# A hybrid layer with 32 experts: four 2 MB weight chunks asked for in uneven row groups, with later pairs, more halves and expert 2's gather later

## What is computed

```
logits = x @ w_router + b_router            (264 x 32)
gates  = softmax(top 4 of logits)
for each expert e, on the tokens that chose it:
    h   = xb @ w_up[e] + b_up[e]            (1024 -> 2048)
    act = min(h_glu, 7) * sigmoid(1.702 * h_glu) * (clip(h_lin, -7, 7) + 1)
    y   = act @ w_down[e] + b_down[e]       (1024 -> 1024)
out = sum over the 4 experts of gate * y
```

## Time and profile before

| | us |
|---|---|
| median of 3 runs | 1084.72 |
| the profiled execution | 1084.98 |
| its span, first to last instruction | 1083.2 |
| TensorE busy | 1065.1 |
| VectorE busy | 361.6 |
| ScalarE busy | 152.6 |
| granted TensorE clock | 0.998 of full speed |
| data moved | 431.47 MB, mean 398 GB/s |

### The profile page before, as it was taken

The page is one execution under the profiler, slowest core; times in us unless marked ns, Lnnn a source line. Parts: engine busy times, 40 slices in busy tenths (PEclk is TensorE's granted clock), DMA queues, the critical chain, the costliest instruction groups (busy, mean ns, idle before and its releaser), DMA issues.

```text
span 1083.2 us, 13206 instructions
## 1 busy us (share of the span) xinstructions
PE 1065.1 (98%) x5687; PEld 442.8 (41%) x5688; DVE 361.6 (33%) x572; ACT 152.6 (14%) x302; POOL 11.9 (1%) x28
## 2 busy tenths in 40 slices
PE   9999999999999999999999999999999999999997
PEld 7888664333333333333333333333333333333332
DVE  3376444233333222233332222333233232232234
ACT  2121144111111111101111111101111111101113
POOL 1000010000000000000000000000000000000002
PEclk9999999999999999999999999999999999999999
DMA  8875969999999999999999999999999999999994
GB/s 284 310 277 207 404 213 389 400 403 433 427 435 429 429 431 431 430 431 431 428 434 429 425 431 427 431 430 430 430 434 428 428 430 429 425 427 427 428 412 173
DMA packets 44075, 431.47 MB, mean 398 GB/s; under 512 B 4808, under 2 KB 20204, under 8 KB 25712
## 3 DMA queue, kind: packets, MB, share of 16 engines
q1 hardware_dynamic: 43408, 430.41, 95.2%
q10 hardware_dynamic: 608, 0.20, 0.1%
HBM read 427.00 MB, written 3.48 MB: 397 GB/s over the span
## 4 chain that ended last, share of the span: by engine, by line
PE 79%; DMA 20%; issue 0%; ACT 0%; DVE 0%; ACTq 0%; POOLq 0%; DVEq 0%; POOL 0%
PE bank L1027 32%; DMA ring_all<-in_w_down 19%; PE bank L1046 17%; PE bank L708 9%; PE bank L1094 5%; PE bank L1001 4%; PE bank L1038 3%; PE bank L818 2%; PE bank L1009 1%; PE bank L1019 1%; PE bank L1106 1%; PE bank L826 1%; DMA ring_all<-in_w_in 1%; PE bank L1087 1%; PE bank L661 1%; PE bank L1132 1%
## 5 line engine op out<-in xcount | busy, mean ns | idle before, releaser
L1027 PE MATMUL bank<-ring_all,work 128*64 128x512 f32 x2040 | 482.4, 600 | 5.8 <-DMA ring_all<-in_w_up 5.8
L1027 PEld LDWEIGHTS bank<-ring_all,work 128*64 128x64 f32 x2040 | 132.5, 136 | 255.0 <-issue 238.8
L1046 PE MATMUL bank<-ring_all,work 128*64 128x512 f32 x992 | 225.6, 596 | 2.7 <-DMA ring_all<-in_w_down 2.6
L1875 DVE TENSOR_TENSOR h_tok<-h_tok,bank 128x1024 f32<-128x1024 f32 (+1 forms) x67 | 81.7, 1220 | 233.7 <-PE bank L1094 227.9
L1046 PEld LDWEIGHTS bank<-ring_all,work 128*64 128x64 f32 x992 | 68.3, 137 | 133.1 <-issue 132.2
L708 PE MATMUL bank<-work,ring_all 128*128 128x264 f32 x384 | 87.0, 387 | 0.5 <-DMA ring_all<-in_w_in 0.5
L1845 DVE TENSOR_TENSOR work<-bank,bias_up 128x1024 f32<-128x1024 f32 x32 | 39.2, 1224 | 127.6 <-PE bank L1038 127.6
L708 PEld LDWEIGHTS bank<-work,ring_all 128*128 128x128 f32 x384 | 72.4, 190 | 12.9 <-DMA ring_all<-in_w_in 0.9
L1094 PE MATMUL bank<-work 64*128 64x512 f32 (+1 forms) x268 | 75.1, 637 | 0.0
L1862 DVE TENSOR_TENSOR work<-work 128x512 f32<-128x512 f32 x32 | 22.2, 693 | 108.9 <-ACT work L1443 108.8
L1427 ACT ACTIVATE work<-bank 128x264 f32<-128x264 f32 x32 | 12.5, 390 | 322.2 <-PE bank L1019 322.2
(11 more groups left out here) (238 smaller groups left out, 549.5 us busy)
## 6 DMA issues: line engine op xcount, KB each, us to landing
ring_all<-in_w_up SPq DMA_DIRECT2D x36, 4096.0 KB, 28.0
ring_all<-in_w_down SPq DMA_DIRECT2D x24, 4096.0 KB, 33.2
ring_all<-in_w_up SPq DMA_DIRECT2D x47, 2048.0 KB, 38.9
ring_all<-in_w_down SPq DMA_DIRECT2D x11, 2048.0 KB, 41.1
ring_all<-in_w_up SPq DMA_DIRECT2D x17, 1024.0 KB, 8.2
ring_all<-in_w_in SPq DMA_DIRECT2D x13, 1024.0 KB, 5.0
ring_all<-in_w_down SPq DMA_DIRECT2D x10, 1024.0 KB, 7.9
ring_all<-in_w_out SPq DMA_DIRECT2D x4, 1024.0 KB, 11.7
```

What stands on the lines that cost most here:

```text
L1027: mm = pe.matmul(bank[half * CAP:(half + 1) * CAP, up_bank(n) + b, :].rearrange("q (k p) -> q p k", k=KT), x, src[half][:, b * 512:(b + 1) ...
L1046: mm = pe.matmul(bank[half * CAP:(half + 1) * CAP, Y, :], av[:, 2 * i + k, :], src[:, k * D + half * 512:k * D + (half + 1) * 512], start= ...
L1875: tt(rows, rows, bank[0:m, b:b + 2, :], ALU.add).then_inc(comb_added, 1)
```

## The change

- Chunks 10 to 23, instead of 10 to 19, come in halves. The semaphores for first halves are now one per slot, with a count.
- Pairs begin at expert 8 instead of expert 4. Experts 4 to 7 are fetched in singles.
- In experts 8, 14, 20 and 26 (`EVENED`) the second chunk of the up projection is asked for in four transfers: rows 0 to 111; rows 112, 114, ... 126; rows 113, 115, 117; rows 119, 121, ... 127. The first chunk of experts 8 and 14 is for that no longer part of a pair (in 20 and 26 it was single already).
- In expert 1's up projection the gather for expert 2 moves from behind step 1 to behind step 6, the turning of the marks of expert 0 from behind step 5 to behind step 4, and the turning of the gathered rows of expert 2 from behind step 3 into the down projection of expert 0, behind step 1. The transposes of the gates move from up(0) to up(2), behind step 0. ScalarE's list follows.

```diff
-HALVES = 10
-PAIRED = (4, 28)
+HALVES = 14
+PAIRED = (8, 28)
 SPLIT = 16
+EVENED = (8, 14, 20, 26)
+EVEN_ROWS = (slice(0, 112), slice(112, 128, 2), slice(113, 119, 2), slice(119, 128, 2))
...
-                 if s % RING < RING - 1 and not (stream[s][0] == "u" and stream[s][1] >= SPLIT and stream[s][2] == 0)]
+                 if s % RING < RING - 1 and not (stream[s][0] == "u" and stream[s][2] == 0
+                                                 and (stream[s][1] >= SPLIT or stream[s][1] in EVENED))]
+        evened = [place["u", e, 1] for e in EVENED]
...
-            seen[s % RING] += 1
+            seen[s % RING] += len(EVEN_ROWS) if s in evened else 1
             signal.append((s % RING, 16 * seen[s % RING]))
...
-            half_in = [sem(f"half_in{i}") for i in range(HALVES + 1)]
+            half_in = [sem(f"half_in{r}") for r in range(RING)]
...
+            halved = [RING - 1] + [s for s in range(RING, RING + HALVES) if s != RING + STASHED]
+
+            def half_signal(s):
+                return s % RING, 16 * sum(h % RING == s % RING for h in halved if h <= s)
...
-                        fill(s, slice(0, 2 * FF), half_in[s - RING + 1])
+                        fill(s, slice(0, 2 * FF), half_in[s % RING])
...
-                    sp.dma_start(ring(s), chunk_src(stream[s])).then_inc(landed[s % RING], 16)
+                    for part in EVEN_ROWS if s in evened else (slice(0, P),):
+                        sp.dma_start(ring(s)[part], chunk_src(stream[s])[part]).then_inc(landed[s % RING], 16)
...
-                    elif n >= 3:
-                        pe.wait_ge(spread_copied, n - 2)
+                    elif n >= 2:
+                        pe.wait_ge(spread_copied, max(n - 2, 1))
...
-                    halved = RING - 1 <= s < RING + HALVES
-                    if half == 0 and halved:
-                        pe.wait_ge(half_in[s - RING + 1], 16)
-                    if half == halved and s - 1 not in pairs:
+                    if half == 0 and s in halved:
+                        r, count = half_signal(s)
+                        pe.wait_ge(half_in[r], count)
+                    if half == (s in halved) and s - 1 not in pairs:
...
                             pe.wait_ge(counted, 1)
-                            pe.wait_ge(gt_ready, 1)
...
-                        if j == (1 if n else 4) and n < E - 1:
+                        if j == (4, 6, 1)[min(n, 2)] and n < E - 1:
                             gather(n + 1)
-                        if j == (3 if n else 6) and n < E - 1:
+                        if j == (6 if n == 0 else 3) and n != 1 and n < E - 1:
                             turn_x(n + 1)
-                        if j == 5 and n > 0:
+                        if j == 4 and n == 1:
+                            turn_marks(0, 2)
+                        if j == 5 and n > 1:
                             turn_marks(n - 1, min(n + 2, E))
...
-                        if j == 6 and n == 0:
-                            pe.wait_ge(bu_ready, 2)
+                        if j == 0 and n == 2:
                             pe.wait_ge(gates_ready, 1)
...
                         if i == 0 and n < E - 1:
                             turn_h(n + 1)
+                        if i == 1 and n == 0:
+                            turn_x(2)
...
+                    if n == 1:
+                        spread_out(0)
                     if n < E - 1:
                         gather_out(n + 1)
-                    if n == 0:
+                    if n == 2:
                         act.wait_ge(gt_psum, 1)
                         nc.scalar.activation(gt[:], bank[0:E, C, 0:T], ACT.Copy).then_inc(gt_ready, 1)
-                    else:
+                    if n >= 2:
                         spread_out(n - 1)
```

More of the change, by code:

```diff
@@ L542, in _ @@
                 sp.wait_ge(wo_psum, 4)
-                fill(FIRST + 2, slice(0, 2 * FF), half_in[0])
+                fill(FIRST + 2, slice(0, 2 * FF), half_in[FIRST + 2])
                 sp.wait_ge(wo_psum, 6)
```

## The result

The changed kernel takes 1125.14 us (median of 6 runs, 1122.48 to 1129.78), the kernel before 1085.17 on the same chip: a ratio of 1.0371 [1.0359, 1.0384], 40 us slower. The forecast was 1080.6 us with a range up to 1083.6; it has the wrong sign, and the loss is over ten times the loss of its worst rival (3.2 us).

What follows compares the result with a forecast made beforehand. The weight stream was taken to set the pace from about 630 us. Terms 1.7 + 0.8 - 0.8 + 2.45 = 4.15 us off 1084.98 gave 1080.8, or 1080.6 against the median; range 1078.9 to 1083.6.

Steps and rivals of the forecast that it cites:

- D: Four uneven chunks, experts 8 to 26: spared engines, taken as the late ones, win 2.45 us; ends 2.45 won, 4.9 lost.
- the sign that the prediction named for D: Last 6 us of the weight stream: DMA share falls steeply from above 0.9 to nothing within some 4 us, no 0.6 shelf.
- The other sign: End of the weight stream: last landing on the chain near 1048.4 us instead of 1052.5; under 2 us refutes the forecast.
- A: Chunks 20 to 23, experts 2 and 3, in halves: closes the 225 to 233 us gap, winning 1.7 us (1.15 to 2.3).
- B: Expert 2's gather, transposes and gate transposes moved: earlier requests at 190 to 200 us win 0.8 us (0 to 1.5).
- Rival 2: Early stream: stalls only move, A and B are lost, C stays lost, D won; 1.65 us faster, 1083.1; chance 0.08.
- C: Smaller rows and singles instead of pairs in the early weight stream cost 0.8 us (0.4 to 1.1).
- E: Extra SP issues, moved TensorE work and new waits: no cost, as TensorE has over 10 us in hand.
- Rival 1: Uneven chunks: evening wins nothing, late engines change from fetch to fetch; A to C win 1.7 us, 1083.0; chance 0.09.
- Rival 3: Uneven chunks: small pieces fall on the late engines, costing 4.9 us; 3.2 us slower, 1087.9; chance 0.06.
- Rival 4: Uneven chunks: 0.4 us fixed cost for each of 12 extra pieces; 0.65 us slower, 1085.4; chance 0.04.

## Why the prediction was wrong

**D, the uneven chunks: the step that failed.** "112 rows are 7 for each of the 16 engines, where 128 rows are 8", so the spared engines win one row of 0.61 us. The count of rows fits the reports (16 + 8 + 3 + 5 engines); the 0.61 us was not right. It came from transfers of 128 rows and was carried over to one of 112 as if a row had a price of its own. While such a transfer is in flight, the engines together work at a half to two thirds of their rate, and rows of whole transfers are held up too: some 10 us a chunk lost, for at most 2.45 us over four chunks to be won. The prediction gave this term two ends, but both (2.45 won, 4.9 lost) were worked out with the same 0.61 us; the trace of before has no transfer with other than 128 rows in this part of the weight stream, and this was the unknown cost to be bounded. The earlier trace rows was of no help: small transfers behind a large one, not a large one over other rows.

Whether anything of the evening came is open. The DMA share at the end of the stream falls faster in the kernel after:

```profile
1100.00:1103.00 3.00, 3.00 (x20) 1.12 (x16) 0.38 (x1) 0.60 (x1) 0.00 (x0) 1.00 1.03 361
1103.00:1106.00 3.00, 3.00 (x18) 1.09 (x16) 1.22 (x1) 0.00 (x0) 0.00 (x0) 1.00 0.81 319
1106.00:1108.00 2.00, 2.00 (x14) 0.59 (x12) 1.22 (x1) 0.00 (x0) 0.00 (x0) 1.00 0.10 40
```

0.81 and then 0.10, where the earlier trace rows has 0.60 and 0.32 and the kernel with whole chunks 0.59 and 0.33. This is the sign that the prediction named for D. But the engines did not come closer together. For the transfer of the earlier trace rows the first and the last report were 8.2 us apart before, 8.8 with the uneven chunks alone and 11.7 in the kernel after. Only the order within changed: 13 reports within 3.7 us of the last with the uneven chunks alone, 9 within 4.1 us before. The other sign, that this transfer lands at about 1048.4 us, failed: it landed at 1093.6. A gain from evening was not measured.

What the partitions have to do with it: the Trainium skill, "SBUF — State Buffer", "Door 1: The DMA port swizzle", says that the bandwidth of a transfer depends on how many of 16 ports its partitions reach, the port being chosen by bits 2 to 4 and 6 of the partition number, and "DMA: Bandwidth & Descriptors", "The descriptor swizzle", that in a transfer to 128 partitions each engine writes one port only. By this 32 or 64 neighbouring partitions reach 8 ports of 16, and rows 0 to 111, if they go out in portions of 7 neighbours, send engines to each other's ports. The number of ports alone is not the rule, though: 112, 96 and 120 rows reach all 16 and are slow, and 16 neighbours reach only 4 and yet have 317 GB/s, no less than the shapes with 8. The measurements agree for 32 and 64 neighbours (305 and 309 GB/s, with some full-rate time in the window), for 16 rows at every eighth or fourth partition (8 ports: 314 and 320), and for the free shapes (435, 433), which reach all 16. The first of these two pages of the Trainium skill goes on that the only way to reach all ports is one transfer that spans all 128 partitions; the transfers of 32 and 64 rows with a step show that not every partition need be in it. I had drawn on the second of the two pages for which engines a piece loads, and not on the first, which speaks against this change.

That engines meet at ports of others is an explanation that fits, not one that was shown: no row of the trace names the engine or port. It would also say why the transfers of 8 rows cost the others something, half of them being sent by engines 0 to 7 to partitions from 64 up. If so, an engine can be spared only where another writes to its port, and evening always pays this price; that was not tried by itself.

**A, the halves.** The gap at 225 to 233 us closed (422 GB/s), but the halves were not what it took: with 10 in place of 14 and late pairs it closes as well (434), as it does with 14 and pairs from expert 5 (418). What counted for the time were the later pairs, which the prediction called "the price of A": with the halves and early pairs the loss just moves to 240 to 290 us (417 against 426 GB/s: 50 x 9 / 430 = 1.0 us), and 1.5 us is what later pairs are worth. The size (1.7) agrees within the noise, its cause was wrong. Rival 2, stalls that only move, is what the halves alone do.

**B, the gather.** Mechanism right, size low: 0.8 was taken, 1.6 measured, which its uncertainty of about 1.5 us does not tell from 0.8. The windows speak for the larger number: 10 x (413 - 339) / 425 = 1.7 us.

**C, the smaller rows.** The rate from 250 to 430 us went from 431 to 429 GB/s with whole chunks, and A to C sum to 2.3 us won where 1.7 was forecast. The cost was not measured by itself: 1.5 + 1.6 - 0.8 = 2.3 fits, but each of the first two is uncertain by its own size. The four terms of the forecast as printed add up to 0.70, unrounded to 0.77, not 0.8; nothing hangs on it.

**E.** Neither the new waits nor SP's issues show: the kernel with whole chunks has all the waits and is faster than the kernel before, and four issues in place of one cost nothing where the rows stand at every fourth partition.

**The rivals.** Rival 1 (1083.0) had evening win nothing and lose nothing; the kernel with whole chunks (1083.8) comes near it, the kernel after does not. Rival 3, the slower case, had the wrong mechanism and a tenth of the size. Rival 4's fixed cost of a piece is small: 112 + 16 rows lose 6.3 and 6.9 us (first, last), 112 + 8 + 3 + 5 lose 7.5 and 7.3, and four transfers of 32 rows at every fourth partition lose none.

## What to carry to other kernels

Before a large transfer is cut by partitions, ask which partitions each part covers, not only how many rows each engine gets: a part that is not spread evenly over all 128 partitions, or has fewer than 32 rows, can slow all engines to half to two thirds of their rate while they look fully busy. If a chunk must be cut, take every second or fourth partition (no loss), or cut it by columns (the control of 14 KB and 2 KB rows lost 0.2 us on the mean of the engines, 1.6 on one). And read GB/s beside the DMA share: a share of 1.0 at 280 GB/s is not a full queue but a slow one.

## What had not been expected of the hardware

- Transfers of 64 neighbouring rows, 8 rows a chunk for every engine, lose 6.7 to 7.6 us per 2 MB, against 4.9 us that such a chunk takes; 64 rows at every second partition lose nothing.
- The source has no part in it, as far as tried: 112 rows read from one 16 KB row are no faster.
- The loss of one uneven chunk grows from 7.3 to 10.0 and 12.1 us along the stream, as the spread of the engines' landings ahead of it grows (2.4, 3.5, 5.3 us): probably the slow transfer is then in flight for longer, and holds up engines that are in others. In the fourth (9.9 us ahead of it) it was 11.4. The cause was not tried.
